# Two gate turns as rounded products of a high and a low part, in a hybrid decoder step on one core

## The chip, the cores and the metric

The kernel runs on one core of a Trainium2 chip. The metric is the device time of one execution in microseconds. TensorE multiplies, VectorE and ScalarE do elementwise work, GpSimd and SyncE mostly issue DMAs; the engines run beside each other and wait for each other by semaphores.

## The reference

One step of a decoder layer for 1024 prompt tokens and 8 new tokens (1032 rows in all, D = 1024), in fp32. Nine conditioning vectors (one for the prompt, eight for the new tokens) give shift, scale and gate by a product with w_ada. What matters here is the gate:

```python
c_act = jax.nn.silu(c)
mod = (c_act @ w_ada[l] + b_ada[l])[:, None, :]
shift, scale, gate = jnp.split(mod, 3, axis=-1)
h = rms_norm(x, g_norm[l]) * (1 + scale) + shift
proj = h @ w_in[l]
# conv branch -> y_a, pool branch -> y_b
m = jax.nn.sigmoid(proj[..., o5:o6]) * y_a + jax.nn.sigmoid(proj[..., o6:]) * y_b
x = x + gate * (m @ w_out[l])
```

So the gate is needed only at the last projection, as nine values for each of 1024 channels.

## The kernel before

Activations lie channel-major: channels on the 128 partitions, 8 tiles of 128 channels, 1032 tokens along the row. Every engine runs a list of instructions written out by hand, and semaphores alone order them against each other; there is no scheduler. Large products are made of fp32 values split in two: a part rounded to the fp32r type, which TensorE multiplies in one pass, and the rest. ScalarE writes the rounded part (hi), VectorE the rest (lo), and TensorE adds hi*hi, hi*lo and lo*hi. Plain jobs (`job`, `k_step`, L1063 to L1074) take 8 steps of nine products of 344 columns; other tiles are done in pairs by a Strassen scheme with items P1 to P7 (`block_product`, L1152), whose sums of activations (`tf`, `tr`) VectorE adds up.

The change lies in the projection w_a_out, jobs JOB_A, JOB_A + 1 and JOB_A + 2 (`single`) and the Strassen items A_ITEMS behind them. Between these jobs TensorE also computes the gate, in two chunks of 512 channels. The names:
- `gate_chunk(n)`, L1296: eight fp32 products of c_act (32 columns wide, at four places of the array) with gate_raw, into the PSUM bank aux[:, n]. The result has the nine vectors on partitions, four times, as four partial sums, and 512 channels along the row. It raises gate_done.
- `gate_out(n)`, ScalarE, L1754: copies aux[:, n] to gate_rows and raises gate_rows_ready.
- `gate_turn(n)`, L1302: with `modulation_turn` (L986) four fp32 products, each with a block of 128 columns of gate_rows as the weights and `pick` (128x9, ones and zeros) as the moving operand. This adds the four partial sums and puts channels on partitions. It raises gate_turned.
- `gate_modulation(n)`, VectorE, L2308: adds the bias into mod, raises gate_ready, for which item P5 waits.

TensorE's order is JOB_A, gate_chunk(0), JOB_A + 1, gate_turn(0), gate_chunk(1), JOB_A + 2, gate_turn(1), items. VectorE's order around it: `merge_a(0)` (which takes JOB_A's result out of PSUM), weights' lo part, two combinations of 128x2064 for the sum P6 (L2371, L2372), `merge_a(1)`, two weight lo parts, two combinations for P4 and P7 (L2378, L2379), the lo part of P6 (L2316), `merge_a(2)`.

Of the kernel before, what the change touches and what calls it, by code (L numbers as in the profile page):

```python
# [23 lines left out]
F32 = mybir.dt.float32  # L24
F32R = mybir.dt.float32r
ACT = mybir.ActivationFunctionType
# [3 lines left out]
P = 128  # L30
# [305 lines left out]
def build(nc, t):  # L336
    with ExitStack() as ctx:
        base = (nc.sbuf_base + 31) // 32 * 32

        def at(name, shape, dt, offset):  # L340
            return nc.alloc_sbuf_tensor_at(name, [P] + shape, dt, offset=offset)
# [84 lines left out]
        scale_b = stage_lo[:, 1, 0:KT]  # L426

        gate_raw = at("gate_raw", [KT, ADA_CHUNK], F32, zone_g + 12 * ROW)
        gate_rows = at("gate_rows", [ADA_CHUNK], F32, ext_at)

        out_tr = [at("out_tr_h", [2, 2, KH, HALF], F32R, zone_h), at("out_tr_b", [2, 2, KH, HALF], F32R, zone_b)]
        out_tf = [at("out_tf_h", [2, 2, KH, HALF], F32, zone_h), at("out_tf_b", [2, 2, KH, HALF], F32, zone_b)]
# [96 lines left out]
        def sem(name):  # L529
            return ctx.enter_context(nc.semaphore(name))  # L530
# [26 lines left out]
        pool_state_stored = sem("pool_state_stored")  # L557
        out_stored = sem("out_stored")

        c_padded = sem("c_padded")  # L560
        c_ready = sem("c_ready")
        ones_ready = sem("ones_ready")
        one_rounded = sem("one_rounded")
# [21 lines left out]
        t_hi_done = sem("t_hi_done")  # L585
        t_lo_done = sem("t_lo_done")
        gate_done = sem("gate_done")
        gate_rows_ready = sem("gate_rows_ready")
        gate_turned = sem("gate_turned")
        gate_ready = sem("gate_ready")  # L590

# [327 lines left out]

        @block.gpsimd  # L920
        def _(pool):
            nc.gpsimd.memset(c_act[:], 0.0).then_inc(c_padded, 1)
            nc.gpsimd.memset(one[:, 0:1], 1.0 / D)
            nc.gpsimd.memset(eps[:, 0:1], RMS_EPS)
            nc.gpsimd.memset(row_mean[:], 0.0)
            nc.gpsimd.memset(pick_half[:, 0:QUAD // 2], 1.0 / D)
            nc.gpsimd.memset(pick_half[:, QUAD // 2:QUAD], 0.0)
            nc.gpsimd.memset(pick_half[:, QUAD:], 1.0 / D)
            nc.gpsimd.memset(eps[:, 1:2], LN_EPS).then_inc(ones_ready, 1)

            def add_row(r):
                pool.wait_ge(y_free, 16 * (r // 2 + 1))
                if r:
                    pool.wait_ge(mean_added, 16 * r)
                pool.dma_start(row_mean[:], t["y_conv"][:, r, :], accum_op=ALU.add).then_inc(mean_added, 16)

            def sum_phase(c, k):

                copied, added = sum_copied[c % 2], sum_added[c % 2]
                base, copies = 64 * (c // 2), 32 * (c // 2) + 32  # L940
                a11, a12, a21, a22 = sum_inputs(c)
                s1, s2, s3, s4 = (sum_output(c, n) for n in range(4))
                if k == 0 and c < 2:
                    pool.dma_start(s1, a21).then_inc(copied, 16)
                    pool.dma_start(s3, a21).then_inc(copied, 16)
                if k == 1:
                    if c >= 2:
                        pool.wait_ge(added, base)
                    if c < 2:
                        pool.wait_ge(copied, copies)  # L950
                    else:
                        pool.wait_ge(sum_first[(c - 2) % 6], 32 * ((c - 2) // 6 + 1))
                    pool.dma_start(s1, a22, accum_op=ALU.add).then_inc(added, 16)  # L953
                    pool.dma_start(s3, a11, accum_op=ALU.add).then_inc(added, 16)
                if k == 2:
                    pool.wait_ge(added, base + 32)
                    pool.dma_start(s2, s1).then_inc(copied, 16)
                if k == 3:
                    pool.wait_ge(copied, copies + 16)
                    pool.dma_start(s2, a11, accum_op=ALU.add).then_inc(added, 16)  # L960
                if k == 4:
                    pool.wait_ge(added, base + 48)
                    pool.dma_start(s4, s2).then_inc(copied, 16)
                if k == 5:
                    pool.wait_ge(copied, copies + 32)
                    pool.dma_start(s4, a12, accum_op=ALU.add).then_inc(added, 16)

            pool.wait_ge(ada_loaded[-1], 16)
            for step in range(3 * SUM_CHUNKS + 3):
                c, k = step // 3, step % 3  # L970
                if c >= 1:
                    sum_phase(c - 1, 3 + k)
                if c < SUM_CHUNKS:
                    sum_phase(c, k)
                if step in MEAN_AT:
                    add_row(MEAN_AT[step])

        @block.tensor
        def _(pe):
# [6 lines left out]
            def modulation_turn(bank, rows, blocks=ADA_BLOCKS):  # L986

                for j in range(blocks):
                    last = nc.tensor.matmul(bank[:, j * NMOD:(j + 1) * NMOD], rows[:, j * P:(j + 1) * P], pick[:], start=True, stop=True)  # L989
                return last  # L990
# [309 lines left out]
                last.then_inc(gate_done, 1)  # L1300

            def gate_turn(n):  # L1302
                pe.wait_ge(gate_rows_ready, n + 1)
                modulation_turn(aux[:, n, :], gate_rows).then_inc(gate_turned, 1)

            single(JOB_A, a_hi, a_lo, before_k=lambda k: pe.wait_ge(a_lo_done, k + 1))
            gate_chunk(0)
# [149 lines left out]
        def _(act):  # L1457
# [10 lines left out]
            nc.scalar.activation(one_r, one[:, 0:1], ACT.Copy).then_inc(one_rounded, 1)  # L1468
            nc.scalar.activation(eps[:, 3:4], eps[:, 0:1], ACT.Silu)
            act.wait_ge(c_loaded, 16)  # L1470
            act.wait_ge(c_padded, 1)
            nc.scalar.activation(c_act[:, :, 0:NMOD], c_in[:], ACT.Silu).then_inc(c_ready, 1)
            nc.scalar.activation(eps[:, 2:3], eps[:, 0:1], ACT.Sqrt)

# [278 lines left out]

            def gate_out(n):  # L1754
                act.wait_ge(gate_done, n + 1)
                nc.scalar.activation(gate_rows[:], aux[:, n, :], ACT.Copy).then_inc(gate_rows_ready, 1)

            def a_t_hi(form, count):
                act.wait_ge(t_summed, 4 + count)
# [145 lines left out]
        def _(dve):  # L1905
# [388 lines left out]
            def merge_a(m, s):  # L2294
                dve.wait_ge(pe_done, s + 1)
                dve.wait_ge(siga_loaded[m % 4], 16 * (m // 4 + 1))
                t_row, m_row = sig_a_row(m), hf[:, KT + m, :]
                v.tensor_tensor(by_chunk(t_row), ps_job(s), by_chunk(t_row), ALU.mult).then_inc(dve_evac, 1)
                dve.wait_ge(dve_evac, s + 1 - JOB_B)
                v.tensor_tensor(m_row, t_row, m_row, ALU.add).then_inc(m_full, 1)  # L2300

            def m_split_lo(m):
# [2 lines left out]
                dve.wait_ge(item_done, LAST + A_AT["P5" if m < KH else "P4", A_B] + 1)  # L2305
                v.tensor_tensor(gr[:, KT + m, :], hf[:, KT + m, :], gr[:, m, :].bitcast(F32), ALU.subtract).then_inc(m_lo_done, 1)

            def gate_modulation(n):  # L2308
                dve.wait_ge(gate_turned, n + 1)
                v.tensor_tensor(mod[:, 4 + n, :, :], aux[:, n, 0:ADA_BLOCKS * NMOD].rearrange("p (j n) -> p j n", j=ADA_BLOCKS),  # L2310
                                wide(ada_b[:, 4 + n, :], NMOD), ALU.add).then_inc(gate_ready, 1)

            def a_t_lo(form, count):
# [57 lines left out]
            link(v.tensor_tensor(full22, br[:, upper_k, second].bitcast(F32), hr[:, upper_k, second].bitcast(F32), ALU.add))  # L2371
            link(v.scalar_tensor_tensor(out=at2, in0=at1, scalar=-1.0, in1=full22, op0=ALU.mult, op1=ALU.subtract))  # L2372
            dve.sem_inc(t_summed, 1)
            merge_a(1, JOB_A + 1)
            item_lo_part(A_SPLIT)
            item_lo_part(A_SPLIT + 1)
            dve.wait_ge(gate_done, 2)
            link(v.scalar_tensor_tensor(out=at4, in0=at2, scalar=-1.0, in1=br[:, upper_k, first].bitcast(F32), op0=ALU.mult, op1=ALU.subtract))  # L2378
            link(v.tensor_tensor(at3, full22, full12, ALU.subtract))  # L2379
            dve.sem_inc(t_summed, 1)  # L2380
# [296 lines left out]
```

## Time and profile before

| | us |
|---|---|
| median of 3 timed runs | 913.08 (912.51 to 913.29) |
| profiled execution, its own time | 912.39 |
| span of its trace, first to last instruction | 910.6 |
| TensorE busy | 898.1 |
| VectorE busy | 805.8 |
| ScalarE busy | 419.0 |

The span is what the trace shows; 1.8 us of the execution lie around it. TensorE's busy time counts matmuls that overlap in the pipeline, so a busy TensorE isn't one at its peak. Of an engine that is idle it matters only whether somebody waits for it. In the rows, PE is the matmul, PEld the weight load, DVE is VectorE, ACT is ScalarE; an fp32 product appears as two records, each with a weight load of its own.

### The profile page before, as it was taken

Reading aid. Unit: us, or ns where it says so; the run is one execution under the profiler, and the core shown is the slowest. Engines: PE = TensorE matmul, PEld = TensorE weight load, DVE = VectorE, ACT = ScalarE, POOL = GpSimd, SP = SyncE. Lnnn points to the kernel's source line nnn. Section 1 sums busy time; section 2 is a strip of 40 time slices with the busy share of each in tenths; the row PEclk is TensorE's granted clock in tenths of the full one; section 3 lists DMA queues with packets and bytes.
Section 4 is the critical chain, followed back from the end, with each engine's and each line's share of the span. In section 5 each row is a group of like instructions: output and inputs, shape, how many; then the busy total and the mean of one; then the engine's idle time right before and its main releaser. Section 6 shows DMA issues by size and latency. Waiting matters only on the chain.

```text
span 910.6 us, 17314 instructions
## 1 busy us (share of the span) xinstructions
PE 898.1 (99%) x7058; PEld 880.6 (97%) x7058; DVE 805.8 (88%) x927; ACT 419.0 (46%) x608; POOL 100.8 (11%) x112
## 2 busy tenths in 40 slices
PE   8999999999999999999999999999999999999996
PEld 4799999999999999999999999999999989999995
DVE  4888999997999995999996899999898798689767
ACT  5773454434453444354443454446444532526452
POOL 0022221101021111111111112000010000000000
PEclk9999999999999999999999999999999999999998
DMA  9969998879688989888989979638987663423515
GB/s 363 364 154 258 254 236 255 240 235 245 174 226 248 253 239 241 227 231 238 282 242 254 242 204 201 214 131 290 369 333 181 225 219 115 141 70 102 167 58 187
DMA packets 86655, 202.77 MB, mean 223 GB/s; under 512 B 12464, under 2 KB 19120, under 8 KB 83376
## 3 DMA queue, kind: packets, MB, share of 16 engines
q1 hardware_dynamic: 53248, 122.76, 38.5%
q0 software_dynamic: 22080, 52.46, 28.7%
q10 hardware_dynamic: 11248, 26.45, 8.3%
q8 instruction: 56, 0.92, 0.4%
q14 instruction: 23, 0.19, 0.1%
HBM read 175.67 MB, written 88.88 MB: 291 GB/s over the span
## 4 chain that ended last, share of the span: by engine, by line
PE 96%; DVE 2%; DMA 1%; issue 0%; SPq 0%; ACT 0%; DVEq 0%
PE ps L1165 23%; PE ps L1161 23%; PE ps L1159 23%; PE ps L1068 8%; PE ps L1073 7%; PE ps L1069 7%; DMA ada_raw<-w_ada 1%; PE ps L983 1%; DVE stage_hi L2565 1%; PE ps L989 0%; DVE hf L2552 0%; PE ps L1362 0%; PE ps L1359 0%; PE ps L1360 0%; SPq L657 0%
## 5 line engine op out<-in xcount | busy, mean ns | idle before, releaser
L2180 DVE SCALAR_TENSOR_TENSOR conv_y<-conv_u,par_all,conv_y 128x1024 f32<-128x1024 f32 x240 | 300.3, 1278 | 2.1 <-DVE conv_y L2166 0.6
L1161 PE MATMUL ps<-tr,hr 128*128 128x258 f32 x824 | 216.4, 283 | 0.0
L1159 PE MATMUL ps<-tr,hr 128*128 128x258 f32 x824 | 215.4, 283 | 0.0
L1592 ACT ACTIVATE hr<-raw 128x512 fp32r<-128x512 f32 (+1 forms) x188 | 115.9, 618 | 113.5 <-PE ps L1165 85.1
L1165 PE MATMUL ps<-tr,hr 128*128 128x258 f32 x824 | 166.3, 283 | 0.0
L1161 PE MATMUL ps<-hr 128*128 128x258 f32 x616 | 161.4, 283 | 0.0
L1159 PE MATMUL ps<-hr 128*128 128x258 f32 x616 | 160.8, 282 | 0.0
L1159 PEld LDWEIGHTS ps<-tr,hr 128*128 128x128 f32 x824 | 156.9, 190 | 0.0
L1161 PEld LDWEIGHTS ps<-tr,hr 128*128 128x128 f32 x824 | 155.6, 189 | 0.0
L2059 DVE TENSOR_TENSOR hr<-raw,hr 128x512 fp32r<-128x512 f32 (+1 forms) x188 | 125.7, 673 | 7.6 <-ACT hr L1592 3.7
L1165 PEld LDWEIGHTS ps<-tr,hr 128*128 128x128 f32 x824 | 127.2, 188 | 0.0
L1165 PE MATMUL ps<-hr 128*128 128x258 f32 x616 | 124.6, 284 | 0.0
L1159 PEld LDWEIGHTS ps<-hr 128*128 128x128 f32 x616 | 117.4, 191 | 0.0
L1161 PEld LDWEIGHTS ps<-hr 128*128 128x128 f32 x616 | 116.3, 189 | 0.0
L1165 PEld LDWEIGHTS ps<-hr 128*128 128x128 f32 x616 | 95.0, 188 | 0.0
L1068 PE MATMUL ps<-gr,w_hi 128*128 128x344 f32 x264 | 84.2, 321 | 0.0
L1069 PE MATMUL ps<-gr,w_hi 128*128 128x344 f32 x264 | 83.8, 320 | 0.0
L1073 PE MATMUL ps<-gr,w_lo 128*128 128x344 f32 x264 | 61.1, 320 | 0.0
L1069 PE MATMUL ps<-hr,w_hi 128*128 128x344 f32 x186 | 58.9, 320 | 0.0
L1068 PEld LDWEIGHTS ps<-gr,w_hi 128*128 128x128 f32 x264 | 49.7, 188 | 0.4 <-DVE w_lo L1917 0.3
L1069 PEld LDWEIGHTS ps<-gr,w_hi 128*128 128x128 f32 x264 | 49.6, 188 | 0.1
L953 POOL DMA_DIRECT2D w_sums<-w_main x15 | 17.2, 1148 | 255.7 <-DMA w_sums<-w_main 255.7
(321 smaller groups left out, 1589.7 us busy)
## 6 DMA issues: line engine op xcount, KB each, us to landing
w_sums<-w_main POOLq DMA_DIRECT2D x64, 512.0 KB, 9.6
raw<-w_sums SPq DMA_DIRECT2D x120, 256.0 KB, 4.6
raw<-w_main SPq DMA_DIRECT2D x94, 256.0 KB, 4.5
w_sums<-w_sums POOLq DMA_DIRECT2D x30, 512.0 KB, 5.8
w_sums<-w_main ACTq DMA_DIRECT2D x26, 512.0 KB, 5.4
w_raw<-w_main SPq DMA_DIRECT2D x16, 512.0 KB, 5.4
ada_raw<-w_ada SPq DMA_DIRECT2D x7, 1024.0 KB, 20.6
sig_a<-stage_hi ACTq DMA_DIRECT2D x8, 516.0 KB, 7.0
```

The lines of the kernel that those rows point to most:

```text
L953: pool.dma_start(s1, a22, accum_op=ALU.add).then_inc(added, 16)
L983: return nc.tensor.matmul(bank[quad, :], c_act[:, k, :], w[:, k, :], start=(k < QUADS), stop=(k >= KT - QUADS), tile_position=(0, k % QUAD ...
L1068: nc.tensor.matmul(out, wh, rhs_hi[:, cols(c)], start=(k == 0), stop=False)
L1069: nc.tensor.matmul(out, wh, rhs_lo[:, cols(c)], start=False, stop=False)
L1073: last = nc.tensor.matmul(ps[:, s_par, c, 0:CW], wl, rhs_hi[:, cols(c)], start=False, stop=(k == n_k - 1))
L1159: nc.tensor.matmul(bank[:, c, :], wh[:, w_cols], x_hi[:, k, t_cols], start=start and k == 0, stop=False, skip_group_check=True)
L1161: nc.tensor.matmul(bank[:, c, :], wh[:, w_cols], x_lo[:, k, t_cols], start=False, stop=False, skip_group_check=True)
L1165: last = nc.tensor.matmul(bank[:, c, :], wl[:, w_cols], x_hi[:, k, t_cols], start=False, stop=(k == n_k - 1), skip_group_check=True)
L1592: nc.scalar.activation(ring(q)[0][:, 0:n], raw5[:, raw_slot(q), 0:n], ACT.Copy).then_inc(item_hi, 1)
L2059: v.tensor_tensor(lo[:, 0:n], raw5[:, raw_slot(q), 0:n], hi[:, 0:n].bitcast(F32), ALU.subtract).then_inc(item_lo, 1)
L2180: ins = v.scalar_tensor_tensor(out=y, in0=conv_u[:, x, k:k + SEQ], scalar=par_all[:, g, x, k:k + 1], in1=y, op0=ALU.mult, op1=ALU.add)
L2565: link(v.reciprocal(row, row))
```

## The change

The fp32 turn of the gate's rows is replaced. ScalarE now writes the rounded part gate_hi (type fp32r) instead of a full copy; VectorE writes gate_lo = aux - gate_hi, also fp32r; TensorE's turn is, for each of the four blocks, one product with gate_hi and one with gate_lo, added in PSUM, with pick_r as the moving operand. pick_r is a rounded copy of pick with a tenth column (its first once more), made by VectorE in two small casts ahead of the first gate_lo; mod is read from columns ten apart. The turn waits for gate_lo_ready. ScalarE's and VectorE's second parts wait for the first turn, since the buffers are used twice; the first gate_lo also waits for y_std_ready, since its buffer held another sum. Apart from that, the wait of ScalarE on c_padded (the zeroed c_act) is removed; it stood behind its wait on ones_ready, which the same GpSimd queue raises later.

```diff
-        gate_rows = at("gate_rows", [ADA_CHUNK], F32, ext_at)
+        gate_hi = at("gate_hi", [ADA_CHUNK], F32R, ext_at)
+        gate_lo = at("gate_lo", [ADA_CHUNK], F32R, at_start)
+        pick_r = at("pick_r", [NMOD + 1], F32R, at_start + 4 * ADA_CHUNK)
...
-            nc.gpsimd.memset(c_act[:], 0.0).then_inc(c_padded, 1)
+            nc.gpsimd.memset(c_act[:], 0.0)
...
             def gate_turn(n):
-                pe.wait_ge(gate_rows_ready, n + 1)
-                modulation_turn(aux[:, n, :], gate_rows).then_inc(gate_turned, 1)
+                pe.wait_ge(gate_lo_ready, n + 1)
+                for j in range(ADA_BLOCKS):
+                    columns = aux[:, n, j * (NMOD + 1):(j + 1) * (NMOD + 1)]
+                    block = slice(j * P, (j + 1) * P)
+                    nc.tensor.matmul(columns, gate_hi[:, block], pick_r[:], start=True, stop=False, skip_group_check=True)
+                    last = nc.tensor.matmul(columns, gate_lo[:, block], pick_r[:], start=False, stop=True, skip_group_check=True)
+                last.then_inc(gate_turned, 1)
...
-            act.wait_ge(c_padded, 1)
...
             def gate_out(n):
                 act.wait_ge(gate_done, n + 1)
-                nc.scalar.activation(gate_rows[:], aux[:, n, :], ACT.Copy).then_inc(gate_rows_ready, 1)
+                if n:
+                    act.wait_ge(gate_turned, n)
+                nc.scalar.activation(gate_hi[:], aux[:, n, :], ACT.Copy).then_inc(gate_hi_ready, 1)
...
+            def gate_split_lo(n):
+                dve.wait_ge(gate_hi_ready, n + 1)
+                if n == 0:
+                    dve.wait_ge(y_std_ready, CHUNKS)
+                    v.tensor_copy(pick_r[:, 0:NMOD], pick[:])
+                    v.tensor_copy(pick_r[:, NMOD:], pick[:, 0:1])
+                else:
+                    dve.wait_ge(gate_turned, n)
+                v.tensor_tensor(gate_lo[:], aux[:, n, :], gate_hi[:].bitcast(F32), ALU.subtract).then_inc(gate_lo_ready, 1)
...
             dve.sem_inc(t_summed, 1)
+            gate_split_lo(0)
             merge_a(1, JOB_A + 1)
             item_lo_part(A_SPLIT)
             item_lo_part(A_SPLIT + 1)
             dve.wait_ge(gate_done, 2)
+            gate_split_lo(1)
```

TensorE at the first turn, before: behind job JOB_A + 1 (L1073) the turn (L989) and the second gate chunk (L983).

```order
L1073 MATMUL ps<-br,w_lo 128x344 x3
L989 MATMUL ps<-pick,gate_rows 128x9 [waits gate_rows_ready]
L989 MATMUL ps<-pick,gate_rows 128x9 x3
L983 MATMUL ps<-gate_raw,c_act 32x512 [waits gate_loaded]
L983 MATMUL ps<-gate_raw,c_act 32x512 x7
L1068 MATMUL ps<-br,w_hi 128x344 [waits dve_evac,w_lo_done]
```

And in the changed kernel, whose lines are numbered differently (L1309 and L1310 are the turn, L985 the chunk):

```order
L1075 MATMUL ps<-br,w_lo 128x344 x3
L1309 MATMUL ps<-pick_r,gate_hi 128x10 [waits gate_lo_ready]
L1310 MATMUL ps<-pick_r,gate_lo 128x10
L1309 MATMUL ps<-pick_r,gate_hi 128x10
L1310 MATMUL ps<-pick_r,gate_lo 128x10
L1309 MATMUL ps<-pick_r,gate_hi 128x10
L1310 MATMUL ps<-pick_r,gate_lo 128x10
L1309 MATMUL ps<-pick_r,gate_hi 128x10
L1310 MATMUL ps<-pick_r,gate_lo 128x10
L985 MATMUL ps<-gate_raw,c_act 32x512 [waits gate_loaded]
L985 MATMUL ps<-gate_raw,c_act 32x512 x7
L1070 MATMUL ps<-br,w_hi 128x344 [waits dve_evac,w_lo_done]
```

Four fp32 products are now eight rounded ones, and the first waits for gate_lo_ready. The second turn reads the same.

VectorE from the two combinations of the P6 sum (L2371, L2372) to the lo part of P6 (L2316), before; L2298 and L2300 are merge_a(1), L2059 the lo parts of the items' weights:

```order
L2371 TENSOR_TENSOR tf<-br,hr 128x2064
L2372 SCALAR_TENSOR_TENSOR tf<-tf 128x2064 [waits dve_chain]
L2298 TENSOR_TENSOR stage_lo<-ps,stage_lo 128x1032 [waits dve_chain,siga_loaded1,pe_done]
L2300 TENSOR_TENSOR hf<-stage_lo,hf 128x1032 [waits dve_evac]
L2059 TENSOR_TENSOR w_lo<-raw_64,w_hi 128x512 [waits item_hi] x2
L2378 SCALAR_TENSOR_TENSOR tf<-tf,br 128x2064 [waits gate_done]
L2379 TENSOR_TENSOR tf<-tf 128x2064 [waits dve_chain]
L2316 TENSOR_TENSOR tr<-tf,tr 128x2064 [waits dve_chain,t_hi_done]
```

And in the changed kernel, where L2391 is L2372, and L2320, L2321 and L2324 are gate_split_lo:

```order
L2390 TENSOR_TENSOR tf<-br,hr 128x2064
L2391 SCALAR_TENSOR_TENSOR tf<-tf 128x2064 [waits dve_chain]
L2320 CAST pick_r<-pick 128x9 [waits dve_chain,y_std_ready,gate_hi_ready]
L2321 CAST pick_r<-pick 128x1
L2324 TENSOR_TENSOR gate_lo<-ps,gate_hi 128x512
L2306 TENSOR_TENSOR stage_lo<-ps,stage_lo 128x1032 [waits siga_loaded1,pe_done]
L2308 TENSOR_TENSOR hf<-stage_lo,hf 128x1032 [waits dve_evac]
L2067 TENSOR_TENSOR w_lo<-raw_64,w_hi 128x512 [waits item_hi] x2
L2324 TENSOR_TENSOR gate_lo<-ps,gate_hi 128x512 [waits gate_turned,gate_hi_ready,gate_done]
L2399 SCALAR_TENSOR_TENSOR tf<-tf,br 128x2064
L2400 TENSOR_TENSOR tf<-tf 128x2064 [waits dve_chain]
L2335 TENSOR_TENSOR tr<-tf,tr 128x2064 [waits dve_chain,t_hi_done]
```

The casts and the first gate_lo stand between the second combination and merge_a(1), the second gate_lo ahead of the combination for P4.

## Rows read from the trace of the kernel before

**Rows 1.** The page: each engine's busy share; shares of the chain that ended last.
```profile
PE 898.1 (99%) x7058; PEld 880.6 (97%) x7058; DVE 805.8 (88%) x927; ACT 419.0 (46%) x608; POOL 100.8 (11%) x112
PE 96%; DVE 2%; DMA 1%; issue 0%; SPq 0%; ACT 0%; DVEq 0%
```

**Rows 2.** The waits of TensorE: waiter, releaser, us in total, times, longest.
```profile
PE ps L996 <- POOL eps L929: 2.2, 1, 2.2
PE ps L983 <- DMA ada_raw<-w_ada: 1.3, 2, 1.1
PE ps L1413 <- DVE tok_hi L2542: 0.9, 1, 0.9
```

**Rows 3.** Timeline of TensorE's products: start us, us, line, out<-in, count.
```profile
745.38 0.95 PE L989 MATMUL ps<-pick,gate_rows 128*128 128x9 f32 x8
746.26 1.93 PE L983 MATMUL ps<-gate_raw,c_act 128*32 128x512 f32 x16
...
759.58 0.95 PE L989 MATMUL ps<-pick,gate_rows 128*128 128x9 f32 x8
```

**Rows 4.** The chain of waits, the piece at the first gate turn.
```profile
745.54 0.79 PE ps L989 x8
```

**Rows 5.** Timeline of VectorE, 745 to 764 us; in brackets the idle time before.
```profile
745.24 2.31 DVE L2372 SCALAR_TENSOR_TENSOR tf<-tf 128x2064 f32<-128x2064 f32 x1
747.77 1.23 DVE L2298 TENSOR_TENSOR stage_lo<-ps,stage_lo 128x1032 f32<-128x1032 f32 x1 [0.22 <-DVE tf L2372]
...
751.39 2.30 DVE L2378 SCALAR_TENSOR_TENSOR tf<-tf,br 128x2064 f32<-128x2064 f32 x1
...
759.78 1.23 DVE L2298 TENSOR_TENSOR stage_hi<-ps,stage_hi 128x1032 f32<-128x1032 f32 x1 [1.29 <-PE ps L1073]
...
763.40 0.29 DVE L2310 TENSOR_TENSOR mod<-ps,ada_b 128x36 f32<-128x36 f32 x2
```

**Rows 6.** Timeline of ScalarE, 741 to 760 us.
```profile
741.63 0.58 ACT L1756 ACTIVATE gate_rows<-ps 128x512 f32<-128x512 f32 x1
...
759.78 1.15 ACT L1592 ACTIVATE w_hi<-raw 128x512 fp32r<-128x512 f32 x2 [8.69 <-PE ps L1073]
```

**Rows 7.** Timeline of TensorE's weight loads at the first gate turn.
```profile
745.22 1.01 PEld L989 LDWEIGHTS ps<-pick,gate_rows 128*128 128x128 f32 x8
```

**Rows 8.** Timeline of TensorE's loads and VectorE, the last products, 900 to 904 us.
```profile
900.09 0.69 PEld L1403 LDWEIGHTS ps<-one,stage_hi 128*86 128x86 f32 x8
...
902.50 0.17 DVE L2542 TENSOR_SCALAR tok_hi<-tok_rstd 86x4 fp32r<-86x4 f32 x1
902.78 0.52 PEld L1413 LDWEIGHTS ps<-eye_r,tok_hi 86*128 86x128 f32 x4 [0.91 <-issue]
...
903.23 0.53 PEld L1413 LDWEIGHTS ps<-eye_r,tok_lo 86*128 86x128 f32 x4
```

**Rows 9.** Groups of VectorE: line, tiles, count, busy us, mean ns, idle before.
```profile
L2333 DVE TENSOR_TENSOR stage_hi<-ps,stage_hi 128x516 f32<-128x516 f32 x1 | 0.7, 689 | 0.0
L2310 DVE TENSOR_TENSOR mod<-ps,ada_b 128x36 f32<-128x36 f32 x2 | 0.3, 183 | 0.0
```

**Rows 10.** Timeline of TensorE's weight loads, the first 12 us.
```profile
3.24 0.34 PEld L996 LDWEIGHTS ps<-one 128*128 128x128 f32 x1 [0.52 <-issue]
4.10 0.34 PEld L996 LDWEIGHTS ps<-one 128*128 128x128 f32 x1 [0.52 <-issue]
...
7.35 0.19 PEld L996 LDWEIGHTS ps<-one 128*128 128x128 f32 x1 [0.36 <-issue]
7.78 0.19 PEld L996 LDWEIGHTS ps<-one 128*128 128x128 f32 x1 [0.24 <-issue]
...
11.75 2.23 PEld L1029 LDWEIGHTS ps<-hf,stage_lo 128*32 128x32 f32 x80 [0.76 <-issue]
```

**Rows 11.** Stretches at the end; the third number from the right is PEclk.
```profile
904.00:905.00 1.00, 0.00 (x0) 0.00 (x0) 1.00 (x2) 0.00 (x0) 0.00 (x0) 0.94 0.45 168
905.00:907.00 2.00, 0.00 (x0) 0.00 (x0) 2.00 (x3) 0.00 (x0) 0.00 (x0) 0.50 0.88 323
```

More of the change, by code:

```diff
@@ L558, in build @@
         out_stored = sem("out_stored")
-        c_padded = sem("c_padded")
         c_ready = sem("c_ready")
@@ L587, in build @@
         gate_done = sem("gate_done")
-        gate_rows_ready = sem("gate_rows_ready")
+        gate_hi_ready = sem("gate_hi_ready")
+        gate_lo_ready = sem("gate_lo_ready")
         gate_turned = sem("gate_turned")
@@ L2306, in m_split_lo @@
                 v.tensor_tensor(gr[:, KT + m, :], hf[:, KT + m, :], gr[:, m, :].bitcast(F32), ALU.subtract).then_inc(m_lo_done, 1)
+            def gate_split_lo(n):
[7 more added lines that the diff above has]
+                v.tensor_tensor(gate_lo[:], aux[:, n, :], gate_hi[:].bitcast(F32), ALU.subtract).then_inc(gate_lo_ready, 1)
             def gate_modulation(n):
                 dve.wait_ge(gate_turned, n + 1)
-                v.tensor_tensor(mod[:, 4 + n, :, :], aux[:, n, 0:ADA_BLOCKS * NMOD].rearrange("p (j n) -> p j n", j=ADA_BLOCKS),
+                v.tensor_tensor(mod[:, 4 + n, :, :],
+                                aux[:, n, 0:ADA_BLOCKS * (NMOD + 1)].rearrange("p (j n) -> p j n", j=ADA_BLOCKS)[:, :, 0:NMOD],
                                 wide(ada_b[:, 4 + n, :], NMOD), ALU.add).then_inc(gate_ready, 1)
```

## The prediction

> **What bounds the kernel now.** I read the page's busy shares and the chain of waits first. TensorE is busy 99% of the span and holds 96% of the chain that ended last; VectorE is busy 88% and holds 2% of it [rows 1]. Then I read who TensorE waits for: the three longest kinds of its waits are 2.2, 1.3 and 0.9 us, and they stand at the start (memsets, the first loads) or after the last products, none near the gates [rows 2]. So a microsecond that TensorE loses in the middle is a microsecond on the end, and no later wait is there to take it back. For the changed place I read the timelines of TensorE, VectorE and ScalarE around the two gate turns, and TensorE's chain there: it runs from the last weight product of job JOB_A + 1 straight into the turn at 745.54 and on, with no gap [rows 3, 4].
>
> **The products themselves.** The edit is meant to shorten the two turns. Before, a turn is four fp32 products, and the trace shows it as eight records with eight weight loads of 128 columns: the first load starts at 745.22, the first record of the next group at 746.26, so a turn takes 1.04 us [rows 3, 7]. After, it is eight rounded products (hi and lo for each of four blocks), again eight loads of 128 columns. The nearest rows are the eight rounded products of the final spread, with one load of 128 columns each and 86 columns to move: the first four go from 902.78 to 903.23, 0.113 us each, and all eight loads together from 902.78 to 903.23 + 0.53 = 903.76, 0.98 us [rows 8]. The fp32 turn's eight loads take 1.01 us [rows 7]. The pace is that of the load in both, and the number of loads is the same. So I take 1.01 - 0.98 = 0.03 us less per turn, 0.06 for both. The bounds: no gain, and the eight narrower loads of 86 columns with one column to move, 0.69 us in all [rows 8], which would make a gain of 0.32 a turn and 0.64 for both. The tenth column, one more to move, is inside these bounds.
>
> A rule of the Trainium skill would price the loads differently. "TensorE: Matmul & The Clock Gate", section "Weight-path perf modes", says that loads of a full set of 128 columns go on a faster path whenever the type is not FP32, with four times less as the theory for the narrowest type and no win for fp32. The rows above let the rounded loads go at the fp32 pace, so the trace speaks against it for this type; what it would make of the time is the third rival.
>
> **The new wait.** The turn now needs both parts, and the lo part is VectorE's. The order puts the first lo part behind the 128x2064 combination that forms the P6 sum (L2372 before) and ahead of the merge of job JOB_A + 1. That combination starts at 745.24, when TensorE is already at the turn, and lasts 2.31 us, to 747.55; the instruction that follows it starts at 747.77, after 0.22 us for the chain [rows 5]. Before, the turn waited for ScalarE's copy alone, done at 741.63 + 0.58 = 742.21, over 3 us early [rows 6]. Now, step by step:
> - Two small casts for pick_r: the trace has two small VectorE instructions in a row, 0.183 us each, that together fill 0.29 us [rows 5, 9], so the second starts 0.11 us after the first. Two steps of 0.11 bring VectorE to 747.99. At worst they go one after the other with their whole length and the extra semaphores cost one more chain wait: 0.15 + 0.22 later.
> - The subtraction of 512 columns, PSUM as one source: 0.69 us as for 516 columns [rows 9], so 748.68.
> - From a VectorE result to TensorE's first load: 902.78 - 902.67 = 0.11 us [rows 8], so the first load at 748.79.
> The load was at 745.22. TensorE is 3.57 us late at the turn. The sum: 3.57 - 0.06 = 3.51 us. From below: with the gain of 0.64, 2.9 us; from above 3.57 + 0.37 = 3.9 us.
>
> **What is queued behind, and whether it adds.** On VectorE: the merge of job JOB_A + 1, two weight lo parts, the second gate lo part, then the work up to the P6 lo part. From 747.77 to 751.39 this took 3.62 us [rows 5]; now it starts at about 748.7 and ends at 752.3. The second lo part waits for ScalarE's second hi, and that for the second gate product: it ended at 746.26 + 1.93 = 748.19 [rows 3], now at 751.7, the copy of 0.58 [rows 6] ends at about 752.4, and the lo part at 753.1. The work up to the P6 lo part took from 751.39 to 758.49 (759.78 less 1.29 idle) [rows 5]: 7.10 us, so it ends at 760.2. The next merge waits for TensorE, which frees it at 759.78 + 3.51 = 763.3: 3 us of slack instead of 1.29. The second turn, at about 763, finds its lo part ten microseconds old. So the second split costs nothing; its cover is the 1.29 us that VectorE sat idle plus the 3.5 that TensorE loses. If the first stall weren't there, VectorE's added 0.2 + 0.69 + 0.69 = 1.6 us would be 0.3 over the 1.29, and even that would only delay a merge that TensorE needs later. On ScalarE the second copy now also waits for the first turn (about 749.8), before the product that it waits for anyway; behind it are weight copies that started at 759.78 after 8.69 us of idle [rows 6]. Nothing is late there. The removed wait on the zeroed c_act costs and gives nothing: ScalarE has first to wait for a later memset of the same queue, and TensorE's first wait of 2.2 us ends on that later one too [rows 2].
>
> **The sum against the clock of the runs.** The profiled execution took 912.39 us (span 910.6). With 3.51 it is 915.9. The median of the timed runs is 913.08, 0.69 above it, so the forecast is 913.08 + 3.51 = 916.6 us, and its own range by the bounds above is 916.0 to 917.0.
>
> **Rivals.**
> 1. The stall costs the clock as well. TensorE has nothing to do from 745.5 to 748.8 and then about 1 us of tiny products. The trace shows one fall: the granted clock is 0.94 of full in 904 to 905 and 0.50 from 905 on, after the sparse products of the end [rows 11], which is the 1.2 GHz level. And it shows what that level costs: at the start the fp32 records begin 0.86 us apart (3.24, 4.10), and from 7.35 on 0.43 apart [rows 10], though the clock column says full there. First work is at 2.2 [rows 2], so 5.0 us went at half pace and lost 2.5 us. Such a fall in the stall would cost between nothing and 2.5 us more: 916.6 to 919.1, its middle 917.8. Against it: the gap lies between two dense stretches, while the tail was sparse for 5 us. Chance 0.20. The same page, section "Why this matters for your kernels", warns of idle gaps between bursts for this reason; no row of this trace shows a fall between two dense stretches.
> 2. The wait is covered, not slower. Mechanism: VectorE reaches the first lo part before TensorE reaches the turn. The point at which it decides is 745.22; it needs VectorE's chain to be 3.5 us ahead of the trace's, and the order puts 2.31 us of combination directly before. Then only the gain of the turns is left, 0.06: 913.0 us. Chance 0.04.
> 3. The rounded loads are fast. If a load of 128 columns went at the pace of the trace's narrow loads, 32 columns, 2.23 / 80 = 0.028 us [rows 10], the eight would take 0.22 us instead of 1.01 and both turns would give back 1.58: 913.08 + 3.57 - 1.58 = 915.1. This is what the skill's rule above amounts to. Chance 0.05.
> 4. The change doesn't do what it says: each rounded product is issued with two loads, as an fp32 one is. Then eight more loads per turn, 16 x 0.113 = 1.8 us: 918.4. The final spread shows one load for each rounded product [rows 8]. Chance 0.02.
>
> **How the numbers follow.** Forecast 0.67, the rivals 0.20, 0.04, 0.05 and 0.02, 0.02 for what I don't see, half on each side. About 0.2% (1.8 us) is what a measurement of this kernel can tell from no change. Slower: 0.67 + 0.20 + 0.05 + 0.02 + 0.01 = 0.95; the same 0.04; faster 0.01. The range 915.5 to 919.1 holds the forecast's and the clock's cases, and leaves out the covered wait and the fast loads.
>
> **What would show it.** The waits of TensorE get a new row, a rounded gate product waiting for gate_lo on VectorE, 3.1 to 3.5 us, once; the combination before it ends at about 747.6 and the first turn's load starts at about 748.8. The second turn has no wait. A turn has eight loads, 0.11 us apart. VectorE's idle time before the third merge grows from 1.29 to about 3. Everything from there on is shifted by one amount. The granted clock between 745 and 760 stays at full, or the first rival holds. Wrong would be: no such wait, a wait under 2 us, a second wait at the second turn, or load spacing well under 0.1.

## The result and the profile after

| | before | after |
|---|---|---|
| median of timed runs, us | 913.12 (912.51 to 914.49, 6 runs) | 918.75 (917.34 to 921.20, 6 runs) |
| profiled execution, us | 912.39 | 917.74 |
| span of the trace, us | 910.6 | 915.9 |
| mean granted clock | 0.997 | 0.995; the six runs 0.991 to 0.995 |

The changed kernel is slower: ratio 1.0064, 95% interval 1.0054 to 1.0074, which is 5.6 us. The forecast was 916.6 with a range of 915.5 to 919.1. The sign and the range held, but 2.1 us are missing from the forecast's sum. The trace shows 1.7 us of clock loss, where the first rival put it; the rest isn't in this execution, which at 917.74 us is the second fastest of the six.

The waits of TensorE in the changed kernel (waiter, releaser, us in total, times, longest; L998, L985 and L1420 are L996, L983 and L1413 of before):

```profile
PE ps L1309 <- DVE gate_lo L2324: 3.1, 1, 3.1
PE ps L998 <- POOL eps L931: 2.2, 1, 2.2
PE ps L985 <- DMA ada_raw<-w_ada: 1.2, 2, 0.8
PE ps L1420 <- DVE tok_hi L2563: 0.9, 1, 0.9
```

Beside [rows 2] there is one new row of size, the one that the prediction named: the turn's first product (L1309) waits once, 3.1 us, for gate_lo on VectorE. TensorE's timeline around it (start, us, line, count; L1075 are the last products of job JOB_A + 1, L985 the second gate chunk, L1070 the next job):

```profile
745.23 0.64 PE L1075 MATMUL ps<-br,w_lo 128*128 128x344 f32 x3
748.97 0.27 PE L1309 MATMUL ps<-pick_r,gate_hi 128*128 128x10 f32 x1 [3.10 <-DVE gate_lo L2324]
...
749.96 3.59 PE L985 MATMUL ps<-gate_raw,c_act 128*32 128x512 f32 x16
753.48 0.43 PE L1070 MATMUL ps<-br,w_hi 128*128 128x344 f32 x1
```

Compare with [rows 3]. In this execution job JOB_A + 1 ends 0.33 us later than in the trace of before (745.23 here, 744.90 there for its last three products), a difference from the start of the kernel. The first load and product come at 748.97; the load was at 745.22 [rows 7]. That is 3.75 us, or 3.42 us without the 0.33. The chunk begins 3.70 us later than before (749.96 against 746.26), so the turn itself changes nothing to speak of. But the chunk's sixteen records now fill 3.59 us; in [rows 3] they fill 1.93. So 1.66 us are lost in the chunk, in which nothing waits.

The stretches from 749 to 757 us of the same trace (the stretch, its length, busy time of PE, PEld, DVE, ACT and POOL, then PEclk, the granted clock in shares of 2.4 GHz, and DMA):

```profile
749.00:750.00 1.00, 1.00 (x12) 0.98 (x15) 1.00 (x1) 1.00 (x2) 0.00 (x0) 0.98 0.00 0
750.00:751.00 1.00, 1.00 (x9) 0.34 (x12) 0.97 (x2) 0.93 (x2) 0.00 (x0) 0.50 0.00 0
752.00:753.00 1.00, 1.00 (x8) 0.00 (x0) 0.53 (x1) 0.00 (x0) 0.00 (x0) 0.50 0.71 78
753.00:755.00 2.00, 2.00 (x13) 1.52 (x10) 0.68 (x2) 0.60 (x1) 0.00 (x0) 0.91 0.95 380
755.00:757.00 2.00, 2.00 (x15) 2.00 (x14) 2.00 (x2) 0.00 (x0) 0.00 (x0) 1.00 0.28 108
```

From 750 the clock is at 0.50, the 1.2 GHz level, and the 0.91 of 753 to 755 says that it came back at about 753.4. It fell 1.0 us after TensorE had taken up its work again, at the end of the eight tiny products (ten columns each). In the trace of before, the stretches 740 to 760 are at 1.00 throughout. For the profiled executions the account up to the next job (L1070 at 753.48, in the trace of before at 748.12) is 0.33 (start) + 3.42 (wait) + 1.66 (clock) - 0.05 (turns) = 5.36, against 917.74 - 912.39 = 5.35.

VectorE's timeline (L2391 is the combination L2372 of before; L2320, L2321 and L2324 are the split; L2306 and L2308 a merge):

```profile
745.57 2.31 DVE L2391 SCALAR_TENSOR_TENSOR tf<-tf 128x2064 f32<-128x2064 f32 x1
748.09 0.17 DVE L2320 CAST pick_r<-pick 128x9 fp32r<-128x9 f32 x1 [0.22 <-DVE tf L2391]
748.17 0.15 DVE L2321 CAST pick_r<-pick 128x1 fp32r<-128x1 f32 x1
748.24 0.68 DVE L2324 TENSOR_TENSOR gate_lo<-ps,gate_hi 128x512 fp32r<-128x512 f32 x1
748.83 1.22 DVE L2306 TENSOR_TENSOR stage_lo<-ps,stage_lo 128x1032 f32<-128x1032 f32 x1
...
754.32 0.69 DVE L2324 TENSOR_TENSOR gate_lo<-ps,gate_hi 128x512 fp32r<-128x512 f32 x1 [1.79 <-PE ps L985]
...
765.13 1.23 DVE L2306 TENSOR_TENSOR stage_hi<-ps,stage_hi 128x1032 f32<-128x1032 f32 x1 [3.11 <-PE ps L1075]
```

The two casts follow each other after 0.08 us and the subtraction after another 0.07, so gate_lo ends at 748.92 and TensorE's load starts 0.05 us later. The second gate_lo waits 1.8 us for the chunk that the low clock stretches. Yet the third merge, at 765.13, still has 3.11 us of idle time before it (1.29 in [rows 5]). ScalarE, start and us, with the idle time before in brackets:

```profile
753.63 0.60 ACT L1764 ACTIVATE gate_hi<-ps 128x512 fp32r<-128x512 f32 x1 [2.70 <-PE ps L985]
765.13 1.15 ACT L1598 ACTIVATE w_hi<-raw 128x512 fp32r<-128x512 f32 x2 [10.91 <-PE ps L1075]
```

Its second gate_hi waits 2.70 us for the chunk and holds up nothing: the weight copies behind it come after 10.91 us of idle time (8.69 in [rows 6]).

The weight loads of the first turn and of the second:

```profile
748.97 0.19 PEld L1309 LDWEIGHTS ps<-pick_r,gate_hi 128*128 128x128 f32 x1 [3.40 <-DVE gate_lo L2324]
749.08 0.19 PEld L1310 LDWEIGHTS ps<-pick_r,gate_lo 128*128 128x128 f32 x1
...
749.75 0.19 PEld L1310 LDWEIGHTS ps<-pick_r,gate_lo 128*128 128x128 f32 x1
...
764.78 0.19 PEld L1309 LDWEIGHTS ps<-pick_r,gate_hi 128*128 128x128 f32 x1
...
765.71 0.19 PEld L1161 LDWEIGHTS ps<-br,w_hi 128*128 128x128 f32 x1
```

Eight loads 0.11 us apart, 0.99 us from the first to the chunk's load in the first turn, 0.93 us in the second. The fp32 turn took 1.04 us [rows 3, 7]. There are as many loads as before, at the same pace.

### The profile page after: what moved, and what is told of

It is laid out like the page before. It is cut to its first block and busy times, and to the rows that moved or that the text cites. A ratio compares the mean times of both kernels' runs of the same rounds, so it can differ in the third digit from the quotient of the medians.

```text
span 915.9 us, 17320 instructions
## 1 busy us (share of the span) xinstructions
PE 899.7 (98%) x7058; PEld 880.4 (96%) x7058; DVE 807.1 (88%) x931; ACT 419.2 (46%) x608; POOL 100.8 (11%) x112
## 5 line engine op out<-in xcount | busy, mean ns | idle before, releaser
L1070 PE MATMUL ps<-gr,w_hi 128*128 128x344 f32 x264 | 84.2, 321 | 0.0
L1075 PE MATMUL ps<-gr,w_lo 128*128 128x344 f32 x264 | 61.1, 320 | 0.0
L1070 PEld LDWEIGHTS ps<-gr,w_hi 128*128 128x128 f32 x264 | 49.7, 188 | 0.4 <-DVE w_lo L1925 0.3
L1075 PEld LDWEIGHTS ps<-gr,w_lo 128*128 128x128 f32 x264 | 45.2, 188 | 0.0
```

The source lines that it names most:

```text
L1070: nc.tensor.matmul(out, wh, rhs_hi[:, cols(c)], start=(k == 0), stop=False)
L1075: last = nc.tensor.matmul(ps[:, s_par, c, 0:CW], wl, rhs_hi[:, cols(c)], start=False, stop=(k == n_k - 1))
```

## The experiments

All times are medians. Each kernel's neighbour is the kernel before, measured beside it on the same chip.

| kernel | TensorE idle at the turn, us | median, us | neighbour, us | over it | 95% interval of the ratio |
|---|---|---|---|---|---|
| the change | 3.1 | 918.75 (6 runs) | 913.12 (6 runs) | 5.6 | 1.0054 to 1.0074 |
| early split | 0 | 913.37 (11) | 912.68 (15) | 0.7 | 0.9996 to 1.0014 |
| change + three products of ones | 0.5 | 916.45 (5) | 912.68 | 3.8 | 1.0031 to 1.0056 |
| change + one product of ones | 2.2 | 917.29 (5) | 912.82 (21) | 4.5 | 1.0039 to 1.0064 |
| before + wait for P6 sum | 2.1 | 916.57 (5) | 912.68 | 3.9 | 1.0032 to 1.0058 |
| before + wait for half the merge | 3.5 | 920.22 (5) | 912.82 | 7.4 | 1.0069 to 1.0097 |
| before + wait for the merge | 4.7 | 920.56 (4) | 912.68 | 7.9 | 1.0073 to 1.0100 |
| change, second chunk ahead of the turn | 1.2 | 915.61 (9) | 913.10 (25) | 2.5 | 1.0014 to 1.0033 |
| hi part alone | 0 | 912.35 (11) | 912.82 | -0.5 | 0.9984 to 1.0001 |
| before without c_padded | 0 | 912.94 (11) | 912.82 | 0.1 | 0.9992 to 1.0009 |
| before + product of ones at the end | 0 | 912.89 (11) | 913.10 | -0.2 | 0.9989 to 1.0006 |
| early split + product of ones at the end | 0 | 912.86 (11) | 913.10 | -0.2 | 0.9989 to 1.0008 |

The theory: the change's loss is the wait for gate_lo, 3.4 us, plus a fall of the granted clock that this wait brings about. The rivals: the rounded products or VectorE's added work cost by themselves; or the part above 3.4 us isn't the clock's.

### The split moved ahead of the combinations

```diff
             split_for(JOB_A)
+            gate_split_lo(0)
             link(v.tensor_tensor(full22, ...
...
             dve.sem_inc(t_summed, 1)
-            gate_split_lo(0)
             merge_a(1, JOB_A + 1)
```

> The changed kernel with the first split of the gate's rows (the two casts and the first gate_lo) moved ahead of the two 128x2064 combinations of the P6 sum on VectorE. ScalarE's gate_hi is ready at 742.54 in the changed kernel's trace, VectorE is free at 743.23, so gate_lo should be there at about 744.0 and TensorE reaches the turn at about 745.5. Theory A (the whole loss is the wait for gate_lo and what follows from it): no wait at the turn, granted clock at full throughout, 913.0 us (2 x 0.05 us gained on the turns). Theory B (the eight rounded products, the tenth column or the added VectorE work cost as well): 913.6 us or more, with a wait at the third merge or at an item.

VectorE's first gate_lo and what follows it (L2391 is in this kernel the first of the two combinations), and TensorE's first turn and chunk (a "..." stands between the two engines):

```profile
743.18 0.68 DVE L2324 TENSOR_TENSOR gate_lo<-ps,gate_hi 128x512 fp32r<-128x512 f32 x1
743.78 2.30 DVE L2391 TENSOR_TENSOR tf<-br,hr 128x2064 f32<-128x2064 f32 x1
...
745.55 0.17 PE L1309 MATMUL ps<-pick_r,gate_hi 128*128 128x10 f32 x1
...
746.43 1.92 PE L985 MATMUL ps<-gate_raw,c_act 128*32 128x512 f32 x16
```

gate_lo ends at 743.86, TensorE runs into the turn at 745.55 without a gap, and the chunk takes 1.92 us. 913.37 us, nothing that can be told from the kernel before (interval 0.9996 to 1.0014), where the change is 5.6 us over its own. So all that the change adds, the eight products, the tenth column, ScalarE's rounding, VectorE's two subtractions and two casts, costs nothing measurable; what costs is the place of three instructions (two casts and a subtraction) in VectorE's list. VectorE is then just in time: its third merge starts at 759.94 with no idle time before it, where [rows 5] have 1.29.

The 0.7 us over its neighbour lie within the interval. The loads of the last products (L1420, the final spread) in this kernel's profiled execution, and a stretch:

```profile
902.94 0.93 PEld L1420 LDWEIGHTS ps<-eye_r,tok_hi 86*128 86x128 f32 x4 [0.91 <-issue]
903.75 0.97 PEld L1420 LDWEIGHTS ps<-eye_r,tok_lo 86*128 86x128 f32 x4
...
903.00:904.00 1.00, 1.00 (x5) 1.00 (x6) 0.81 (x2) 0.00 (x0) 0.00 (x0) 0.50 1.01 344
```

They take 0.93 and 0.97 us, 0.52 and 0.53 in [rows 8], all eight 1.78 us instead of 0.98: here the clock fell as they began, in the trace of before behind them [rows 11]. In this one execution (913.40 us) that is 0.8 us.

### Products of ones in the gap

```diff
+            pe.wait_ge(dve_evac, JOB_A + 1 - JOB_B)
+            keep_warm(3, width=WARM_WIDE)
             gate_turn(0)
```

> The changed kernel with three fp32 products of 512 columns of ones ahead of the first turn, into a PSUM bank that the next job overwrites; they take 3 x 0.86 = 2.6 us of the 3.1 us that TensorE otherwise waits. Theory A (wait of 3.5 us plus a fall of the clock): the wait shrinks to about 0.5 us, the first turn starts where it did, the clock stays at full in every run, and the time is 913.1 + 3.5 = 916.6 us, some 2 us less than the changed kernel although TensorE does more. Theory B (the time above 916.6 isn't the clock's): no change from 918.8.

The wait in front of the products of ones is for a merge that ended long before: their result goes to a PSUM bank that must be free. TensorE's products of ones and first turn product, and the stretches around:

```profile
746.21 2.75 PE L998 MATMUL ps<-one 128*128 128x512 f32 x6
749.49 0.27 PE L1309 MATMUL ps<-pick_r,gate_hi 128*128 128x10 f32 x1 [0.53 <-DVE gate_lo L2326]
...
746.00:749.00 3.00, 2.96 (x9) 1.16 (x7) 2.75 (x5) 0.52 (x1) 0.00 (x0) 1.00 0.71 229
749.00:750.00 1.00, 0.51 (x5) 0.51 (x5) 1.00 (x2) 1.00 (x1) 0.00 (x0) 1.00 0.01 4
750.00:760.00 10.00, 10.00 (x70) 8.54 (x70) 9.68 (x8) 2.04 (x4) 0.00 (x0) 1.00 0.31 105
```

The turn waits 0.53 us instead of 3.10, starts when VectorE is ready as before, and the clock is 1.00 in all three stretches. 916.45 us, where 916.6 was expected. This is close to the forecast's own sum, 3.5 us over before: TensorE does 2.6 us more work than in the changed kernel, and the kernel is 3.8 us over its neighbour instead of 5.6. The rival without the clock, 918.8, falls: it lies above the interval, which ends at 917.8. One of the five runs was 918.73 at a mean clock of 0.994 where the profiled one had 0.997. No trace shows where its clock was low, so the expectation of a full clock in every run isn't shown.

With one product of ones in place of three:

```diff
+            keep_warm(1, width=WARM_WIDE)
             gate_turn(0)
```

> The changed kernel with one fp32 product of 512 columns of ones (0.86 us) ahead of the first turn, so that TensorE's idle time there is about 2.2 us instead of 3.1; the turn starts where it did. Theory A (any idle time of 2 us there is enough for the clock to fall, as in the kernel that waited 2.1 us): no or little gain, 918 or more, clock at half for some us. Theory B (the fall depends on the length of the idle time and three products were more than needed): 916.5.

```profile
748.56 0.27 PE L1309 MATMUL ps<-pick_r,gate_hi 128*128 128x10 f32 x1 [2.21 <-DVE gate_lo L2326]
...
748.00:749.00 1.00, 0.44 (x4) 0.45 (x5) 1.00 (x2) 1.00 (x1) 0.00 (x0) 1.00 0.00 0
749.00:750.00 1.00, 1.00 (x10) 0.98 (x13) 0.97 (x2) 1.00 (x3) 0.00 (x0) 0.59 0.00 0
752.00:753.00 1.00, 1.00 (x8) 0.00 (x0) 0.11 (x1) 0.00 (x0) 0.00 (x0) 0.70 0.78 235
```

The idle time is 2.21 us, the clock falls at about 749.2, in the middle of the turn, and is back at about 752.6. The median is 917.29, between the two theories; of five runs three are above 917.2 with clocks of 0.992 to 0.995, and one is 915.85 at 0.997. So 2.2 us is not safe. That a shorter gap costs less than the change's is a tendency: the intervals overlap, and the low stretch of this trace, 3.4 us, is as long as the change's.

### The wait alone, in the kernel before

```diff
+            pe.wait_ge(t_summed, 6)
             gate_turn(0)
```

> The kernel before, with its fp32 turn, whose first turn also waits for VectorE's sum of P6 (counted at 747.6 in the trace of before), so TensorE is idle for about 2.1 us at the turn and starts its loads 2.4 us later. Theory A (delay plus clock, where the fall comes only with a long enough idle time): +2.4 us, 915.5, clock at full in all or most runs. Theory B (any wait there costs the same clock loss of about 2 us): 917.5 us. Theory C (a wait of this size is taken back later): under 914.5.

TensorE's fp32 turn and chunk, and stretches behind them:

```profile
748.42 1.06 PE L989 MATMUL ps<-pick,gate_rows 128*128 128x9 f32 x8 [2.08 <-DVEq L2374]
749.41 2.58 PE L983 MATMUL ps<-gate_raw,c_act 128*32 128x512 f32 x16
...
750.50:751.00 0.50, 0.50 (x8) 0.00 (x0) 0.50 (x2) 0.50 (x2) 0.00 (x0) 0.54 0.00 0
752.00:753.00 1.00, 1.00 (x4) 1.00 (x5) 1.00 (x2) 0.60 (x1) 0.00 (x0) 0.50 0.85 211
753.50:754.00 0.50, 0.50 (x3) 0.50 (x3) 0.50 (x1) 0.00 (x0) 0.00 (x0) 0.54 0.91 358
```

The fp32 turn waits 2.08 us and the clock still falls, at about 750.5 and thus later than in the change, and is back at about 753.9: the chunk takes 2.58 us instead of 1.93, and the first products of the next job are slow too. The first loads are about 2.4 us late, and the median is 3.9 us up, which leaves 1.5 us for the clock. The trace is of the slowest of the five runs (918.00 us; the fastest took 915.75). I had taken 915.5, with the clock at full after so short a gap, for likelier. That was wrong; theory B's mechanism was right, its price too high.

```diff
+            pe.wait_ge(dve_evac, JOB_A + 2 - JOB_B)
             gate_turn(0)
```

> The kernel before, with its fp32 turns, whose first turn also waits for the first half of the merge of job JOB_A + 1 (done at 749.0 in the trace of before), so its first load starts about 3.9 us later than before; the change's own delay was 3.4 to 3.6. Theory A (the change's loss is this delay and the clock, and the kind of product doesn't matter): 3.9 us plus 2 to 2.5 us for the clock, 918.8 to 919.4, a trace like the changed kernel's with the clock at half from about 750 on. Theory B (rounded products or the split itself add to the loss): at most 917.5.

```profile
749.00 1.70 PE L989 MATMUL ps<-pick,gate_rows 128*128 128x9 f32 x8 [3.49 <-DVE stage_lo L2299]
750.63 3.64 PE L983 MATMUL ps<-gate_raw,c_act 128*32 128x512 f32 x16
...
749.00:750.00 1.00, 1.00 (x6) 1.00 (x6) 1.00 (x1) 1.00 (x3) 0.00 (x0) 0.61 0.00 0
...
756.00:757.00 1.00, 1.00 (x8) 1.00 (x7) 0.96 (x2) 0.00 (x0) 0.00 (x0) 0.97 0.00 0
```

Here the wait is 3.49 us, near the change's 3.10, with fp32 products and without any split, and the first load is 3.8 us late. The time is 7.4 us up, more than the change's 5.6. So neither the rounded products nor the split are needed for the loss, and theory B (at most 917.5) falls. My expectation of 918.8 to 919.4 was too low as well: the clock fell at 749.2, so that the turn's loads too went slowly (records fill 1.70 us, 0.95 in [rows 3]) and the chunk's 3.64, and it was back only at 756.1. In all five runs the mean clock was 0.991 or 0.992. The low stretch of 6.8 us is twice the change's; at half pace it costs, by estimate, 3.4 us, which with the 3.8 us of delay gives 7.2 of the 7.4 us.

```diff
+            pe.wait_ge(m_full, 2)
             gate_turn(0)
```

> The kernel before, with its fp32 turn, whose first turn also waits for the end of the merge of job JOB_A + 1 (about 750.3 in the trace of before), so TensorE's loads start 5.2 us later. Theory A (delay plus clock): a fall of the clock in every run, 5.2 us plus about 1.7 to 3 us: 920.0 to 921.3. Theory B (delay alone): 918.3, clock at full.

```profile
750.36 1.87 PE L989 MATMUL ps<-pick,gate_rows 128*128 128x9 f32 x8 [4.75 <-DVE hf L2301]
752.17 3.64 PE L983 MATMUL ps<-gate_raw,c_act 128*32 128x512 f32 x16
```

The wait is 4.75 us and the delay of the first load 5.1 us. The median is 920.56 us, 7.9 us up, 2.8 of them the clock's, within what was expected. The stretch 749 to 750 is at 0.99 and 750 to 751 at 0.50: here the clock fell at 750.0, 0.4 us before TensorE took up its work, and it was back at about 756.8. A gap 1.2 us longer than the last one costs only 0.5 us more in all. The clock's part isn't proportional to the gap.

### The order turned round on TensorE

```diff
-            gate_turn(0)
             gate_chunk(1)
+            gate_turn(0)
```

> The changed kernel with TensorE's order at the place turned round: the second gate chunk (1.9 us of dense products) ahead of the first turn. TensorE reaches the turn at about 747.1 instead of 745.2 and gate_lo is there at about 748.8, so it is idle for some 1.5 us and job JOB_A + 2 starts 1.7 us later than in the kernel before instead of 3.5. Theory A (the fall of the clock needs a sparse stretch of the length of wait and turn together, 4 us in the changed kernel; here 2.5): clock at full, 914.6 us beside 912.9. Theory B (an idle time of 1.5 us with the sparse turn behind it is enough): some runs 1 to 2 us above that, 915 to 916.5. Theory C (the order on ScalarE, whose second copy waits for the first turn, brings a new wait): a row of waits at the second turn or at the third merge.

```profile
745.36 1.92 PE L985 MATMUL ps<-gate_raw,c_act 128*32 128x512 f32 x16
748.52 0.28 PE L1309 MATMUL ps<-pick_r,gate_hi 128*128 128x10 f32 x1 [1.24 <-DVE gate_lo L2324]
...
749.43 0.40 PE L1070 MATMUL ps<-br,w_hi 128*128 128x344 f32 x1
```

The chunk covers 1.9 us of the wait, which shrinks to 1.24 us, and the next job starts at 749.43 instead of 748.12: 1.3 us late, or 1.4 counted from the end of job JOB_A + 1. In the profiled execution, the fastest of nine, the clock stays full, and its time is 913.69 us. But the median of nine runs is 915.61, from 913.69 to 916.93, and only three of the nine are at 914.3 or less, with mean clocks of 0.996 and 0.997; the others have 0.994 to 0.996 (the neighbour's 25 runs have 0.994 to 0.997, so the mean clock alone decides nothing). That is what theory B expects, that a gap of 1.2 us with the tiny products behind it can be enough; but no trace of a slower run shows the fall, and the lower end of the interval, 1.3 us, is the delay alone. No new wait showed on ScalarE or at the merges (theory C).

### Half the loads

The lo products and parts are left out, so that the gate is rounded; the two casts for pick_r stand early on VectorE, and the turn waits for them and for ScalarE's gate_hi.

```diff
-                    nc.tensor.matmul(columns, gate_hi[:, block], pick_r[:], start=True, stop=False, ...)
-                    last = nc.tensor.matmul(columns, gate_lo[:, block], pick_r[:], start=False, stop=True, ...)
+                    last = nc.tensor.matmul(columns, gate_hi[:, block], pick_r[:], start=True, stop=True, ...)
```

> Both turns with the rounded hi part alone: the lo parts and their products are left out (the gate is then rounded), the casts for pick_r stand early on VectorE, and the turn waits for ScalarE alone. Each turn has four loads of 128 columns instead of eight. Theory A (a turn costs its loads, 0.11 us each, whatever the type): 0.45 us less per turn than eight loads, 0.9 us in all, so 912.2 us beside a kernel before of 913.1. Theory B (a turn costs something else, such as the change of shape or the first load's latency): within 0.3 us of the kernel before.

The weight loads of the first turn and of the chunk:

```profile
745.24 0.57 PEld L1310 LDWEIGHTS ps<-pick_r,gate_hi 128*128 128x128 f32 x4
745.83 0.16 PEld L985 LDWEIGHTS ps<-gate_raw,c_act 128*32 128x32 f32 x8
```

Four loads take 0.57 us, and the chunk's first load comes 0.59 us after the turn's first, where eight loads and the step to the chunk take 0.99. That is 0.40 per turn. The median is 912.35, 0.5 us below its neighbour (interval 0.9984 to 1.0001) and 1.0 below the early split with all eight loads, though that one has another neighbour. The profiled executions of the two, in both of which the clock had fallen before or at the last products, are 1.05 us apart (913.40 and 912.35), and 0.16 of these stand already at the first turn's first load. The sign fits theory A, and the trace shows the loads' price; the times alone don't settle it.

### The removed wait, and the last products

The kernel before without c_padded:

```diff
-            act.wait_ge(c_padded, 1)
```

> The kernel before with only the removal of ScalarE's wait on the zeroed c_act. Theory A (that wait never ended last): no change, within 0.3 us of the kernel before. Theory B (one semaphore less at the start lets the first products begin earlier): up to 0.3 us less, with TensorE's first wait shorter than 2.2 us.

912.94 us beside 912.82, TensorE's first wait 2.2 us as before: no change.

Then one more product of ones (256 columns) behind the last token sums, in the kernel before and in the one with the early split:

```diff
             token_columns(2, bf[:, KT - 2, :], start=False)
+            keep_warm(1, 1, 0, width=WARM_COLS)
```

> The kernel before with one more fp32 product of 256 columns of ones (0.4 us) behind the last token sums, where TensorE waits 0.9 us for VectorE before the eight products of the final spread. Theory A (the two groups among the times of one kernel, about 912.5 and 913.4, come from the clock falling before or after these last products): fewer runs in the upper group, median down by up to 0.4 us. Theory B (the groups have another source): no change, 912.9.

> The changed kernel with its first split moved ahead of the P6 combinations (no wait at the turn) and with the same added product of ones behind the last token sums. Theory A (early split costs nothing, the difference of 0.7 us to the kernel before was the clock at the end): within 0.3 us of the kernel before, and below the 913.4 that the early split had alone. Theory B (the early split costs 0.5 us or more by VectorE's added work): 913.4 or more.

The kernel before with it: 912.89 beside 913.10 us (interval 0.9989 to 1.0006). Its highest run is 913.47, while its neighbour's 25 go up to 914.66; a tendency, no more. The early split with it: 912.86 beside 913.10 (0.9989 to 1.0008), so nothing speaks for a price of VectorE's added work. That the 0.7 us of the early split alone were the clock at the end is not shown by the times, since the added product changed the kernel before by nothing that can be told. No version here beats the kernel before by more than can be measured.

## Why the prediction was right, and where it wasn't

- **What bounds, and that no wait is there to take the stall back**: right. The delay at the turn is found undiminished at the end of the span.
- **The products.** Forecast 0.03 us less per turn; the trace gives 0.05 and 0.01 (1.04 to 0.99, 0.94 to 0.93). The rows of the final spread were the right ones: one load per rounded product, 0.11 us each. The third rival, that the rounded loads go at the faster path of "Weight-path perf modes" in the Trainium skill's page "TensorE: Matmul & The Clock Gate", did not happen: the loads are 0.11 us apart. Nor did the fourth: a turn has eight loads.
- **The new wait.** Forecast 3.57 us at the first load, measured 3.42. Two steps were a little too long: the casts (0.11 us each, measured 0.08 and 0.07) and the way from VectorE to TensorE's load (0.11, measured 0.05). The wait itself, 3.1 us, is at the lower end of the 3.1 to 3.5 named.
- **What is queued behind**: right in effect. The third merge had 3.11 us of slack (forecast about 3), the second turn no wait. VectorE's 1.8 us for the second gate_hi wasn't foreseen; it comes from the slow chunk.
- **The removed wait**: nothing, as said.
- **The clock: this is the step that failed.** The forecast took the full clock for likeliest and gave the fall a chance of 0.20, with the argument that the gap lies between two dense stretches while the tail, where the trace showed its one fall, was sparse for 5 us. Both dense stretches were there and the clock fell nevertheless, to 0.50 from 750.0 to 753.4. The argument left out that nothing in the trace of before said how much idle time is harmless. Whether the turn behind the gap, 1 us of tiny products, has a part in it stays open: every gap here had the turn behind it. The traces show falls with gaps of 2.1 us and more, and the spread of the runs speaks for some with 1.2 us. The price was also a little low: between nothing and 2.5 us with a middle of 1.2. The trace has 1.66 us, the median 5.6 - 3.4 = 2.2 us, and the highest run, 921.20 at a clock of 0.991, lies outside the range; the slow level can last longer than the 5.0 us of the start that I took for its bound, as the 6.8 us of the kernel with the 3.5 us wait show.
- So the predicted 916.6 is about the time of the kernel with the clock held by products of ones (916.45). The forecast's own range, 916.0 to 917.0, missed 918.75. The stated range held because it reached over the first rival, which had a chance of 0.20: its cost was weighed, its coming true was not expected.

What stays open is what decides how long the low level lasts from one run to the next. The traces show 3.4 us in the change, with one product of ones and with the wait for the P6 sum, and 6.8 us with the two longer bare waits. Nor does any run separate the length of the gap from the moment at which it falls, or the gap from the tiny products behind it. The six runs of the change, with mean clocks of 0.995, 0.995, 0.993, 0.993, 0.991 and 0.991 in the order of their times, suggest low stretches of different length in one and the same kernel; only the trace of the second fastest exists.

## What to carry to other kernels

When an edit replaces one producer of TensorE's operand by two, look first at what stands ahead of the second one in its engine's own list: here the same three instructions some 5 us earlier turned a loss of 5.6 us into none that can be measured. For products with few columns count weight loads, not passes: a rounded hi and lo product together need as many loads as one fp32 product, and gain nothing. And price a stall of 2 us or more on a busy TensorE with the clock behind it: here such stalls, all with tiny products behind them, took 1.1 us or more on the median on top of the delay. If the stall can't be removed, dense work in it helps; three products of ones took the loss from 5.6 to 3.8 us.

## What the runs showed of the hardware that I had not expected

- A gap of 2.1 us in otherwise dense work was followed by a stretch at the 1.2 GHz level, and its fall came after work had resumed: at 750.5, some 2 us after the turn's first product, in that kernel; at 750.0, 1.0 us after, in the change. With the longest gap, 4.75 us, it fell 0.4 us before work resumed.
- The low stretch lasted 3.4 us in three traces and 6.8 us in two, though TensorE was busy in it without a gap in all but the last of the five.
- In the slow stretch the tiny products slowed down too: eight records of a turn fill 1.70 us instead of 0.95, the last spread's loads 0.93 instead of 0.52. The pace of a weight load follows the granted clock.
- The Trainium skill's page "TensorE: Matmul & The Clock Gate", section "Why this matters for your kernels", advises against idle gaps between bursts. This case's traces agree with the advice, but show the fall already with gaps of 2.1 and 2.2 us, shorter than the one that the page names as the limit; here the measurement decides.
